# Hybrid state-space and stick-breaking layer on one core: two turnings taken off TensorE, and the new tokens' outputs formed in one product per half

## The reference, cut to what matters

```
proj = rmsnorm(x, norm_g) @ w_in      # 2048 -> u_a, z_a, q, k, v, z_b, g_a, g_b
# state space, 64 groups of 16 channels, 64 complex states each
bu = einsum('blgc,gpc->blgp', u, b_bar);  bu[:, 0] += a_bar * h0
h  = associative_scan(a_bar, bu)
y  = real(einsum('blgp,gcp->blgc', h, c)) + D * u
# attention, 8 heads of 128
z  = q @ k.T * SCALE + bias
later = cumsum(log_keep, reverse=True) - log_keep
w  = where(valid, exp(log_sigmoid(z) + later), 0);  o = w @ v
merged = sigmoid(g_a) * (y_a @ w_branch_a) + sigmoid(g_b) * (o @ w_branch_b)
return rmsnorm(x + merged @ w_out), k, v, h_last
```

## Time and profile before

| | |
|---|---|
| median of 3 runs (lowest, highest) | 2921.88 us (2920.22, 2922.9) |
| the profiled execution | 2922.41 us, its span 2920.6 us |
| granted TensorE clock, mean over the span | 0.997 |
| TensorE busy | 2877.1 us (99%) |
| VectorE, ScalarE, GpSimd busy | 1408.9, 996.0, 436.1 us |
| chain that ended last | 89% TensorE, 3% DMA, 2% each GpSimd, SyncE's queue and VectorE |

### The profile page before, as it was taken

One profiled execution on the slowest core, in us unless ns is written; L12 is line 12 of the kernel. 1 busy time (PEld: TensorE's weight loads), 2 busy tenths in 40 slices (PEclk: granted clock), 3 DMA queues, 4 the chain that ended last, 5 costly groups with the idle time before them and its releaser, 6 DMA issues.

```text
span 2920.6 us, 48013 instructions
## 1 busy us (share of the span) xinstructions
PE 2877.1 (99%) x18532; PEld 2828.8 (97%) x18532; DVE 1408.9 (48%) x2628; ACT 996.0 (34%) x1215; POOL 436.1 (15%) x1119
## 2 busy tenths in 40 slices
PE   6999999999999999999999999999999999999998
PEld 5999999999999999999999999999999999999987
DVE  7625454463545455355454534535566543422256
ACT  6235225313522631442253144125422421211142
POOL 7500330330042033004103300500000000000000
PEclk9999999999999999999999999999999999999999
DMA  6233333333433333333333333333558754332273
GB/s 188 69 110 111 106 86 104 108 82 100 127 87 100 101 107 81 107 112 98 102 100 102 87 100 119 83 102 111 173 164 289 242 186 153 102 122 72 79 251 126
DMA packets 448497, 354.31 MB, mean 121 GB/s; under 512 B 83330, under 2 KB 401170, under 8 KB 446482
## 3 DMA queue, kind: packets, MB, share of 16 engines
q1 hardware_dynamic: 448274, 351.36, 40.5%
HBM read 250.34 MB, written 88.34 MB: 116 GB/s over the span
## 4 chain that ended last, share of the span: by engine, by line
PE 89%; DMA 3%; POOL 2%; SPq 2%; DVE 2%; issue 1%; ACT 1%; POOLq 0%; DVEq 0%; ACTq 0%
PE acc L1907 77%; PE acc L2181 5%; PE side L2037 2%; PE side L2054 2%; DMA t_sig_ga<-work 1%; PE side L1874 1%; DMA w_raw<-in_w_branch_a 1%; POOL prologue L1234 1%; SPq L529 1%; PE side L2007 1%; PE side L2008 0%; DMA work<-work 0%; POOL prologue L1235 0%; PE side L2093 0%; PE side L2025 0%
## 5 line engine op out<-in xcount | busy, mean ns | idle before, releaser
L1907 PE MATMUL acc<-x_high,w_high 128*128 128x344 f32 (+1 forms) x5312 | 1708.7, 322 | 3.8 <-DVE w_low L1451 2.4
L1907 PE MATMUL acc<-x_high,w_low 128*128 128x344 f32 (+1 forms) x5312 | 1689.5, 318 | 0.0
L1907 PE MATMUL acc<-x_low,w_high 128*128 128x344 f32 (+1 forms) x5312 | 1689.0, 318 | 0.0
L1907 PEld LDWEIGHTS acc<-x_high,w_high 128*128 128x128 f32 x5312 | 998.0, 188 | 6.3 <-issue 4.0
L1907 PEld LDWEIGHTS acc<-x_low,w_high 128*128 128x128 f32 x5312 | 998.0, 188 | 1.1
L1907 PEld LDWEIGHTS acc<-x_high,w_low 128*128 128x128 f32 x5312 | 997.4, 188 | 0.0
L1451 DVE TENSOR_TENSOR w_low<-w_raw,w_high 128x1024 fp32r<-128x1024 f32 x233 | 288.2, 1237 | 559.3 <-ACT w_high L971 556.6
L971 ACT CAST w_high<-w_raw 128x1024 fp32r<-128x1024 f32 x232 | 243.1, 1048 | 921.8 <-PE acc L1907 830.3
L1327 POOL COPY work<-s_tables 128x28 f32 x16 | 3.3, 208 | 1418.2 <-DVE work L1616 1169.7
L1630 DVE TENSOR_SCALAR work<-side,sb_bias_all 128x128 f32<-128x128 f32 (+3 forms) x64 | 52.3, 818 | 164.9 <-PE side L2054 164.8
L1036 ACT ACTIVATE work<-work 128x128 f32<-128x128 f32 (+3 forms) x64 | 43.7, 683 | 240.0 <-DVE work L1640 240.0
(11 more groups left out here) (334 smaller groups left out, 2615.5 us busy)
## 6 DMA issues: line engine op xcount, KB each, us to landing
w_raw<-in_w_in SPq DMA_DIRECT2D x160, 512.0 KB, 4.1
w_raw<-in_w_out SPq DMA_DIRECT2D x48, 512.0 KB, 4.0
work<-t_sig_ga SPq DMA_DIRECT2D x24, 516.0 KB, 4.4
out<-work SPq DMA_DIRECT2D x22, 512.0 KB, 3.7
t_sig_gb<-stage SPq DMA_DIRECT2D x16, 516.0 KB, 5.1
t_sig_ga<-stage SPq DMA_DIRECT2D x16, 516.0 KB, 4.9
t_sig_ga<-work SPq DMA_DIRECT2D x16, 516.0 KB, 6.2
work<-t_sig_gb SPq DMA_DIRECT2D x16, 516.0 KB, 3.5
```

Source lines behind the costliest of these rows:

```text
L1907: ins = mm(acc[s][:, a, 0:n], w[b][:, kk, :], x[:, kx, c0:c0 + n], start=start, stop=stop)
```

## The change

- Step BT of TensorE is gone in both halves, with ScalarE's copy of B1T. VectorE turns M1 in 32x32 blocks at step 7 or 23 (`B_TURN`), SyncE writes the tile to memory (`b_out`), waits for it, and reads it back in four DMAs (`b_back`), which TensorE waits for at PQ. For the first half both stand ahead of `u_groups`. For the second `b_out(1)` ends chunk 6 and `b_back(1)` begins chunk 7.
- Block 7 of the attention weights goes the way of the others: VectorE turns it at step 75, `w_blocks(7)` at `cn` 19 brings it to another tile (`wT_last`), ahead of `s5_params(0)`. TensorE's step at 78 and the copy are gone.
- At YS one product of all 64 rows of C with all 32 states (128x32) stands for the four; it is written on 64 partitions for each half. At YT VectorE masks out the groups that do not belong together, sums, and adds. The step YN is gone. A further small load brings the 64 columns of C, and three small VectorE instructions ahead of the rounds make the mask.
- In the last round the eight loads of y are spread over chunks 17, 18 and 19, and one splitting step is moved by one.

```diff
+    t_b = dram("t_b_turned", [P, HG * P])
...
-    B1T = c.take(512).rearrange("p (g s) -> p g s", g=HG)
+    B1T_flat = c.take(512)
+    B1T = B1T_flat.rearrange("p (s g) -> p g s", g=HG)
...
-    ysT = c.take(P, NEW)
+    new_parts = c.take(HG * NEW).rearrange("p (g b) -> p g b", g=HG)
+    new_sum = c.take(NEW)
+    C_seeds = c.take(HG * GC)
     fo = c.take(P, HG)
     B0T = c.take(P)
+    m_turned_tile = c.take(512)
     c.at = WORK - (12 * HG + 6 * HG + NEW)
...
+    wT_last = k_blocks
...
+                sp.dma_start(C_seeds, t_n[0][:, bass.ds(g0 * GC, HG * GC)]).then_inc(n_in, 16)
...
+            def b_out(hf):
+                sp.wait_ge(b_turned, i * 2 + hf + 1)
+                sp.dma_start(t_b, m_turned_tile).then_inc(b_sent, 16)
+
+            def b_back(hf):
+                sp.wait_ge(b_sent, i * 32 + 16 * (hf + 1))
+                for j in range(4):
+                    sp.dma_start(B1T_flat[j * 32:(j + 1) * 32].rearrange("a (q n) -> a q n", q=4),
+                                 t_b.rearrange("(q a) n -> a q n", a=32)[:, :, j * P:(j + 1) * P]).then_inc(b_in, 16)
+
...
             def w_blocks(qb):
                 n = qb + 1
-                sp.wait_ge(wt_in, i * 448 + qb * 64 + PRIMED)
+                sp.wait_ge(wt_in, i * 512 + qb * 64 + PRIMED)
                 sp.wait_ge(w_tr, i * 8 + qb + 1)
                 flat = t_w.rearrange("p n -> (p n)")[0:P * n * P].rearrange("(p n) -> p n", p=P)
                 sp.dma_start(flat, w_turned_tile[:, 0:n * P]).then_inc(w_sent, 16)
-                sp.wait_ge(w_sent, i * 112 + (qb + 1) * 16 + PRIMED)
-                if qb:
+                sp.wait_ge(w_sent, i * 128 + (qb + 1) * 16 + PRIMED)
+                into = wT if qb < 7 else wT_last
+                if 0 < qb < 7:
                     sp.wait_ge(pv_mm, i * 8 + qb)
+                elif qb == 7:
+                    sp.wait_ge(ktok_ready, i + 1)
                 for j in range(4):
-                    sp.dma_start(wT[j * 32:(j + 1) * 32, 0:n * P].rearrange("a (q n) -> a q n", q=4),
+                    sp.dma_start(into[j * 32:(j + 1) * 32, 0:n * P].rearrange("a (q n) -> a q n", q=4),
                                  flat.rearrange("(q a) n -> a q n", a=32)[:, :, j * n * 32:(j + 1) * n * 32]).then_inc(wt_in, 16)
...
-                if cn == CHUNKS - 1 and not last:
-                    s5_params(0)
+                if cn == CHUNKS - 1:
+                    w_blocks(7)
+                    if not last:
+                        s5_params(0)
                 if cn == 2:
+                    b_out(0)
+                    b_back(0)
                     u_groups()
                 if cn == 3:
                     toeplitz(0)
@@ -609,7 +636,9 @@
                     s5_seeds(1)
                     y_rows(0)
                     s5_states(0)
+                    b_out(1)
                 if cn == 7:
+                    b_back(1)
                     toeplitz(1)
...
                 if cn == 17 and last:
                     sp.wait_ge(y_sent, FT * 16)
                     sp.wait_ge(chunk_used, GLU0 - 2 + PRIMED)
-                    for t in range(FT):
+                    for t in range(4):
+                        load_y(t)
+                if cn == 18 and last:
+                    for t in range(4, 6):
+                        load_y(t)
+                if cn == 19 and last:
+                    for t in range(6, FT):
                         load_y(t)
...
-    TURN, BT, KM, PQ, SCAN, ROT, YM, YS = (4, 20), (8, 24), (11, 27), (13, 30), (15, 32), (17, 34), (18, 36), (19, 37)
-    YN, YT = 38, 40
+    TURN, B_TURN, BT, KM, PQ, SCAN, ROT, YM, YS = (4, 20), (7, 23), (8, 24), (11, 27), (13, 30), (15, 32), (17, 34), (18, 36), (19, 37)
+    YT = 40
-    WT = (51, 54, 58, 62, 66, 70, 74, 78)
+    WT = (51, 54, 58, 62, 66, 70, 74, 75)
...
                     if p == BT[hf]:
-                        act.wait_ge(b_mm, 2 * i + hf + 1)
-                        nc.scalar.copy(B1T, side[:, 0, :].rearrange("p (g s) -> p g s", g=HG)).then_inc(bt_ready, 1)
+                        act.wait_ge(m_ready, 2 * i + hf + 1)
+                        if hf == 0:
+                            act.wait_ge(oz_ready, 8 * i + PRIMED)
                         nc.scalar.copy(B0.rearrange("p (g c) -> p g c", g=HG), M1[:, :, 0:2 * GC]).then_inc(b0_ready, 1)
                     if p == KM[hf]:
                         act.wait_ge(k_mm, 2 * i + hf + 1)
                         act.wait_ge(b0_ready, 2 * i + hf + 1)
+                        act.wait_ge(b_turned, 2 * i + hf + 1)
                         nc.scalar.copy(Kt[:, :, 7 * GC:15 * GC], side[0:GC, 0, :].rearrange("p (g q) -> p g q", g=HG)).then_inc(kt_ready, 1)
...
-                        nc.scalar.copy(ysT[:, hf * 64:(hf + 1) * 64], side[0:NEW, 1, 0:64])
                         nc.scalar.copy(SO, side[0:HG * NEW, 0, 0:P]).then_inc(ys_ready, 1)
...
-                    if p == WT[qb] and qb == 7:
-                        act.wait_ge(w_tr, 8 * i + qb + 1)
-                        act.wait_ge(pv_mm, 8 * i + 7)
-                        nc.scalar.copy(wT[:, 0:w], side_flat[:, 0:w]).then_inc(wt_ready, 1)
...
-                pool.wait_ge(n_in, i * 64 + 32 * (hf + 1))
+                pool.wait_ge(n_in, i * 96 + 48 * (hf + 1))
...
+        step(V.tensor_reduce(group_rows[:, :], ident[:, :].rearrange("p (g c) -> p g c", c=GC), axis=AX.X, op=ALU.add))
+        step(V.tensor_copy(own_group[0:64, :], group_rows[0:64, 0:HG]), V.tensor_copy(own_group[64:128, :], group_rows[64:128, HG:2 * HG]))
...
+                    if p == B_TURN[hf]:
+                        dve.wait_ge(m_ready, 2 * i + hf + 1)
+                        if hf == 0:
+                            dve.wait_ge(oz_sent, i * 16 + PRIMED)
+                        V.transpose(m_turned_tile.rearrange("p (j b g) -> p j g b", b=32, g=HG), m_flat[:, 0:512].rearrange("p (g j a) -> p j g a", g=HG, a=32)).then_inc(b_turned, 1)
                     if p == KM[hf]:
                         dve.wait_ge(k_mm, 2 * i + hf + 1)
                         dve.wait_ge(b0_ready, 2 * i + hf + 1)
+                        dve.wait_ge(b_turned, 2 * i + hf + 1)
...
                 if p == YT:
-                    dve.wait_ge(yt_mm, i + 1)
-                    V.scalar_tensor_tensor(xy[:, SEQ:TOK], u_off[:, :, NCH], dcol[:, bass.ds(i, 1)], side[:, 0, 0:NEW], ALU.mult, ALU.add).then_inc(yt_ready, 1)
+                    dve.wait_ge(ys_mm, 2 * i + 2)
+                    ch(V.tensor_tensor(new_parts, side[:, 1, 320:320 + HG * NEW].rearrange("p (g b) -> p g b", g=HG),
+                                       own_group[:, :].unsqueeze(2).broadcast_to([P, HG, NEW]), ALU.mult))
+                    ch(V.tensor_reduce(new_sum, new_parts.rearrange("p g b -> p b g"), axis=AX.X, op=ALU.add))
+                    V.scalar_tensor_tensor(xy[:, SEQ:TOK], u_off[:, :, NCH], dcol[:, bass.ds(i, 1)], new_sum, ALU.mult, ALU.add).then_inc(yt_ready, 1)
...
+                if p == WT[7]:
+                    dve.wait_ge(w_ready, 8 * i + 8)
+                    dve.wait_ge(w_sent, i * 128 + 112 + PRIMED)
+                    V.transpose(w_turned_tile, zb[1].rearrange("p (k j a) -> p j k a", j=4, a=32)).then_inc(w_tr, 1)
...
                 for hf in range(2):
-                    if p == BT[hf]:
-                        pe.wait_ge(m_ready, 2 * i + hf + 1)
+                    if p == KM[hf]:
+
+                        pe.wait_ge(n_ready, 2 * i + hf + 1)
                         if hf == 0:
                             pe.wait_ge(oz_ready, 8 * i + PRIMED)
                         else:
                             pe.wait_ge(ys_ready, 2 * i + 1)
-                        for g in range(HG):
-                            last_op = tr(side[:, 0, g * P:(g + 1) * P], M1[:, g, :], ident[:, :])
-                        last_op.then_inc(b_mm, 1)
-                    if p == KM[hf]:
-
-                        pe.wait_ge(n_ready, 2 * i + hf + 1)
-                        pe.wait_ge(bt_ready, 2 * i + hf + 1)
                         for g in range(HG):
                             last_op = one(side[:, 0, g * P:(g + 1) * P], M1[:, g, :], N1[:, g, 0:CH * GC])
...
                         pe.wait_ge(kt_ready, 2 * i + hf + 1)
+                        pe.wait_ge(b_in, (2 * i + hf + 1) * 64)
...
-                        for g in range(HG):
-                            one(side[0:NEW, 1, g * GC:(g + 1) * GC], hn[:, g, :], N1[:, g, 0:GC])
+                        one(side[hf * 64:(hf + 1) * 64, 1, 320:320 + HG * NEW], C_seeds, hn_flat)
                         tr(side[0:HG * NEW, 0, 0:P], hn_flat, ident[:, :]).then_inc(ys_mm, 1)
-                if p == YN:
-                    pe.wait_ge(ys_ready, 2 * i + 2)
-                    one(side[:, 0, 0:NEW], ysT, ident[0:NEW, 0:NEW]).then_inc(yt_mm, 1)
                 for qb in range(8):
-                    if p == WT[qb] and qb == 7:
-                        pe.wait_ge(w_ready, 8 * i + qb + 1)
```

(27 more changed lines are left out.)

12 lines of the change are left out of this document (6 added, 6 removed).

## The result

The changed kernel takes 2959.64 us (median of four runs, 2954.16 to 2965.5) against 2921.86 (2920.22 to 2922.9): a ratio of 1.0128, 95% interval 1.0111 to 1.0145. It is slower by 37.8 us; 25 were forecast. The profiled execution took 2956.37 us, its span is 2954.3.

The account below looks back on a forecast made before the run. TensorE, 99% busy, was taken as the bound, at the end of SyncE's chain from u_groups to YM. 2922.4 + 37.2 - 12.1 = 2947.5 us, 2947 as median; range 2934 to 2966.

Parts of the forecast that it names:

- The forecast of the chain: First half, u_groups to YM: SyncE's delay of 5.1 us passes whole to L1581 and YM, without slack.
- The likeliest case: Chain shifted whole, clock down at most in a few rounds: 2936 to 2957 us, chance 0.58.
- The shift of 5.1 us a round: M1's trip ahead of u_groups issues t_u at 842.3 instead of 837.22; eight rounds make 40.8 us.
- The fit of the Trainium skill: About 2.0 us per DMA plus bytes at 436 GB/s: 2.6 us for 256 KB, some 5 us more over the rounds.
- Start to YM: First halves: 40.8 us less 1.1, 0.5 and 2.0 absorbed in the first round, a cost of 37.2 us.
- Clock, a rival: TensorE's clock falls in the new YM waits: 14 to 55 us over eight rounds, 2961 to 3002 us, chance 0.17.
- Savings: TensorE groups removed: BT 1.8, block 7 6.3, YN 3.0, last round's wait 1.0; sum 12.1 us.
- The last round: Its 1.5 us wait for a turned block of attention weights shrinks, by between 0 and 1.5; 1.0 us taken.
- Block 7's trip: Weights land at 807.2, before TensorE's PV of block 7 at 808.8: hidden with 1.6 us spare, cost 0.
- Rival 1: M1's trip is hidden and only the savings stay, first-half BT added: 2907 us; hidden, faster has chance 0.09.

Follow-up runs that it names:

- e7: The changed kernel with spare products in part of TensorE's first-half waits, at PQ and YM: 2952.46 us, ratio 1.0104 to the kernel before.
- e4: The changed kernel with VectorE turning M1 in the first half right behind the first of the five powers: 2918.78 us, ratio 0.9991 to the kernel before.
- e5: The changed kernel with first-half M1 turned behind the first power and B1T packed by four scattering writes: 2911.14 us, ratio 0.9958 to the kernel before.
- e1: The changed kernel with M1 turned by TensorE again and copied by ScalarE, the rest as changed: 2910.78 us, ratio 0.9964 to the kernel before.
- e3: The kernel before with only B1T stored with the group index fastest, TensorE still turning M1: 2934.68 us, ratio 1.0045 to the kernel before.
- e2: The kernel before with only M1's turning moved to VectorE and its trip through memory to SyncE: 2969.95 us, ratio 1.0165 to the kernel before.
- e6: The changed kernel with u_groups ahead of M1's write and reads in SyncE's first-half order: 2948.12 us, ratio 1.0086 to the kernel before.

## Why the prediction was right, and where it missed

The forecast of the chain held: SyncE's work was shifted whole, most of the shift reached YM, and the kernel is slower. The likeliest case as I had written it held only in part. It said that the clock would be down at most in a few rounds, with 2936 to 2957 us; the clock fell in six of the eight rounds, and 2959.6 lies above that. It is inside the whole range from 2934 to 2966.

- *The shift of 5.1 us a round.* `t_u` is issued 5.9 us later relative to its round's start in the seven rounds after the first, and the rotation ends 5.1 us later in the mean (3.5 to 6.2). That the 5.1 is met so well is in part luck: two errors cancel. The trip is longer than its sum, for the turning takes 1.10 us and not 0.71, since its output is strided, and begins 0.24 us behind the powers; write and reads were 2.03 and 1.76, for 2.03 and 1.74 in the earlier trace rows. The fit of the Trainium skill that the prediction sets beside this ("DMA: Bandwidth & Descriptors", section "Anatomy of one DMA"), 2.6 us, is given for DMAs that GpSimd issues; these are SyncE's. And the chain had some slack where I saw none: from `t_u` to Toep's first DMA it was 10.39 us before and is 9.67 now (858.53 to 868.20). In the first round the shift is 3.5, so 1.6 us were absorbed there, not 2.0. Start to YM came to 37.7 us for 37.2, and low clock is probably in it: YM comes 5.9, 5.8 and 5.0 us later in the three rounds with a fall behind the wait at PQ, and 3.5 to 4.9 in the other four after the first.
- *Strided weights, missed.* The forecast took PQ's products as unchanged, although the diff shows B1T's index order turned round. +7.4 us in the second halves. In the first halves it is hidden: VectorE's copy waits for Toep, whose landing lets it start at 874.84, long after TensorE's products began at 868.68, and TensorE itself stands waiting at YM. This is the largest part of the miss.
- *Clock, a rival and not the forecast.* I priced falls in all eight rounds at 14 to 55 us. They came in six, 27.3 us at the lower level, and cost 5 to 7 us by e7, less than the 1.7 us for each round that was my lower price. The three falls behind waits at YM cost 2.7 (the long one), 1.6 and 1.5 us from YM to YS, together about the +5.7 of the table. Behind the waits at PQ TensorE has another wait ahead of it, at YM, which hides a part. The Trainium skill ("TensorE: Matmul & The Clock Gate", section "HAM oscillation — how this bites in real kernels") says that waits between bursts bring the clock down in each of them; here that held in six rounds of eight.
- *Savings.* Three of them were priced too low by the same rule. I counted a group to the start of the next large matmul, but the one behind that is late too. The large matmul ahead of block 7's transposes and the second behind them, and the same two for YN, in the kernel before (what stands between is in the earlier trace rows):

```profile
805.70 0.32 PE L1907 MATMUL acc<-x_high,w_low 128*128 128x344 f32 x1
...
806.89 0.32 PE L1907 MATMUL acc<-x_low,w_high 128*128 128x344 f32 x1
...
931.80 0.31 PE L1907 MATMUL acc<-x_high,w_low 128*128 128x344 f32 x1
...
932.63 0.32 PE L1907 MATMUL acc<-x_low,w_high 128*128 128x344 f32 x1
```

From the large matmul ahead of the group to the second one behind it, 805.70 to 806.89, are 1.19 us. Without the group they would be two steps of 0.16, so it costs 0.88; 0.90 was gained in seven rounds, where I had 0.79. YN costs 0.52 by the same count (931.80 to 932.63), and YS's two wide instructions 0.06 less than the eight; together 0.58, as measured, where I had taken YN's busy time, 0.38. BT costs 0.45; capped by POOL, 0.31 us a round came of it, where I had 0.22.
- *The last round.* The wait of 1.5 us for the weights stayed, 1.7. What went there was another wait, ahead of block 7's transposes, which the kernel before has in its list and I had not used:

```profile
PE side L2025 <- DVE work L1616: 1.3, 1, 1.3
```

- *Block 7's trip* is hidden in the seven ordinary rounds, as forecast. Rival 1 (hidden, 2907) fell for the kernel as changed, but a trip in a better place comes near its number: e4 2918.8, e5 2911.1.

Added up, measured less forecast: 0.5 (start to YM) + 5.7 (YM to YS) + 7.4 (PQ) - 0.7 (YS to KM) - 1.6 (YN, YS) - 1.2 (block 7, last round) = 10.1 us over the forecast of the rounds; -1.4 us lie outside them. The median of 2959.6 stands 3.3 us over the profiled run, where the forecast took 0.5 off: 10.1 - 1.4 + 3.3 + 0.5 = 12.5, which is the miss of 12.6.

By the experiments 40.9 of the trip's 48.9 us are its place in SyncE's order, with the waits and the low clock that follow from it (e4). The other 8.0, between e4 and e1, are a balance: the strided layout costs more than that (13.0 alone, in e3), and the transposes that TensorE no longer makes give a part back.

## What to carry to other kernels

Before work is moved from the busiest engine to a transfer, write down what stands behind it in the issuing queue and whether the data could be ready earlier: the same trip cost 41 us more behind the five powers than behind the first of them, three steps earlier. Price a small group between large products to the second large product behind it. Read every changed index order in a diff as a change of the operands' strides, and look who reads with them. When the bound engine gets faster, name the next one: here POOL's stretch gave back part of what the packing had won until KM was moved behind it.

## What the runs showed of the hardware

- A weight load of 128 columns of fp32 takes 191 ns packed, about the same at 8 bytes from element to element (eight entries of PQ 1.09 us for 1.05), and about 327 ns at 16 bytes, which holds TensorE up by 117 ns a load (eight entries 1.98 us).
- Behind a small group the first two large matmuls start 0.24 us apart and not 0.16.
- VectorE's 32x32 turning of 128x512 fp32 takes 0.71 us with packed output and 1.10 us where the output steps by 16 bytes.
- Waits of 1.7 to 3.4 us of a TensorE that is otherwise busy were followed by 3.4 or 6.8 us at half clock in most rounds, but not in all: two of 2.84 and 2.60 us were not. The changed kernel's four runs lie 11 us apart, but e2 and e6, whose clock falls in six rounds as well, lie 5 and 3 us apart in theirs, so the scatter is not shown to come from it.
